# Two transformer blocks on one core: three weight strips interleaved behind four of the norms instead of two, and the fourth strip split earlier

## Chip, cores and metric

The kernel runs on one NeuronCore of a Trainium2 chip. The metric is device time in microseconds (us) for one launch. The engines are named as in the profile: PE (TensorE), DVE (VectorE), ACT (ScalarE), POOL (GpSimd) and SP, whose queue issues the weight transfers.

## The reference

One launch computes two blocks in float32 on 512 tokens of width 1024. What matters here is that four large products each follow a root-mean-square norm directly:

```python
# first block
x = x + merged @ w_mix_out
u = rmsnorm(x, norm_ffn_w)                       # norm "ffn0"
up, gate = split(u @ w_ffn_up)
x = x + (silu(causal_dwconv(up)) * gate) @ w_ffn_down
# second block, x = rmsnorm(x, norm_final_w)
h = modulate(rms_norm(x, g_ffn1), sh1, sc1)      # norm "ffn1"
x = x + 0.5 * (1 + ga1) * swiglu(h, w1_gate, w1_up, w1_down)
h = modulate(rms_norm(x, g_mix), sh2, sc2)       # norm "mix2"
x = x + (1 + ga2) * hybrid_mixer(h, w_in, b_f, g_q, g_k, w_o)
h = modulate(rms_norm(x, g_ffn2), sh3, sc3)      # norm "ffn2"
x = x + 0.5 * (1 + ga3) * swiglu(h, w2_gate, w2_up, w2_down)
```

## The kernel before

Activations are kept transposed: 8 chunks of 128 features by 512 tokens. Every weight matrix is cut into strips of 128 output columns. One strip is one *unit* `u`, and the units of the whole program are numbered in one list, `UNITS`; `U[...]` gives the first unit of a stage. A float32 product is made from three matmuls in fp32r: weights and activations are each split into a high and a low part, and `three` issues high times high, high times low and low times high. A unit with 8 chunks is therefore 24 matmuls of 128x512 into one bank of PSUM.

Each unit passes through a ring of four slots (`SLOTS`): SP loads it into `w_raw` once the unit four earlier has ended (`unit_done`), ACT rounds it into `w_hi` (`cut_hi`), DVE subtracts to get `w_lo` (`cut_lo`, which counts `lo_cut` up), and PE waits on `lo_cut`. ACT and DVE run their instructions in the written order, so a `cut_hi` or `cut_lo` stands between other work of theirs.

The result of unit `u` goes to bank `u % 2` (`ubank`). Before it starts in that bank, PE waits on `bank_read[u % 2]` until the unit two earlier has been read out. Who reads depends on the stage. Behind ffn0, ACT copies the first strip of a pair to `t_a`, DVE runs a causal convolution of three instructions on it (`conv`), ACT applies SiLU, and then DVE multiplies with the second strip (`t_b<-t_b,ps`), which frees the second strip's bank. Behind ffn1 and ffn2, ACT applies SiLU to the first strip and DVE multiplies with the second. Behind mix2 the strips are `gate_f`, then the first query strip `p0`, then the first key strip `p0+1`, the value strip `p0+2`. ACT copies `gate_f` to `t_b`, loads another function table, and casts the two halves of `p0` to `q_hi`; DVE then makes `q_lo` in two instructions and frees the bank of `p0`. PE turns the copy of `gate_f` with four transposes between `p0+1` and `p0+2`.

A norm goes over the 8 chunks: DVE makes `t_b`, ACT makes `u_hi`, DVE makes `u_lo`. Behind the four norms above, PE does not wait for all chunks: `unit_pair` takes the first two strips side by side, so each chunk that arrives feeds 6 matmuls. The third and fourth strip follow one after the other as ordinary units. Small filler matmuls (`keep_busy`) run while PE waits for the norm. Bank 7 (`AUX`) holds the sum of squares that the norm's root is made from (`rstd_set` tells that it was read). In the ffn0 stage DVE also takes chunks of the modulation weights (`mod_chunk`, `mod_acc<-mod_raw`), whose transfers SP issues between the strips (`MOD_AT`).

Of one norm, the strips are called u0, u0+1, u0+2 and u0+3 below.

Of the kernel before, what the change touches and what calls it, by code (L numbers as in the profile page):

```python
# [18 lines left out]
KC = D_MODEL // P  # L19
# [41 lines left out]
AUX = 7  # L61
# [29 lines left out]
U = {}  # L91
# [41 lines left out]
FILL = {"mix": 0, "ffn0": 1, "ffn1": 2, "mix2": 3, "heads": 4, "ffn2": 5}  # L133
SQ = {"ffn0": 0, "ffn1": 1, "mix2": 2, "ffn2": 3}
# [43 lines left out]
def two_blocks(nc, d, out):  # L178
    ctx = ExitStack()
    with ctx:  # L180
# [3 lines left out]
        def sem(name):  # L184
            return ctx.enter_context(nc.semaphore(name))


        w_hi = [sb(f"w_hi{n}", [P, KC, P], F32R) for n in range(SLOTS)]
        with ExitStack() as r0:
            w_raw = [sb(f"w_raw{n}", [P, KC, P], F32, r0) for n in range(SLOTS)]  # L190
        with ExitStack() as r0:
            w_lo = [sb(f"w_lo{n}", [P, KC, P], F32R, r0) for n in range(SLOTS)]
# [26 lines left out]
        u_hi = sb("u_hi", [P, KC, SEQ], F32R)  # L219
        u_lo = sb("u_lo", [P, KC, SEQ], F32R)  # L220
# [45 lines left out]
        ps = ctx.enter_context(nc.psum_tensor("ps", [P, 8, SEQ], F32))  # L266
# [19 lines left out]
        squared, summed, total_done, rstd_set = (sem(n) for n in ("squared", "summed", "total_done", "rstd_set"))  # L286
        normed, u_hi_set, u_lo_set = (sem(n) for n in ("normed", "u_hi_set", "u_lo_set"))
# [30 lines left out]
        def bank(b):  # L318
            return ps[:, b, :]

        def ubank(u):

            return ps[:, {U["w_o"] + 2: 3, U["w_o"] + 3: LATE_BANK}.get(u, u % 2), :]

# [80 lines left out]
        def scalar(e):  # L405
# [25 lines left out]
            def norm(which, first_unit, groups=0):  # L431
                cut_hi(first_unit + 2)
                root(which)
                if groups:
                    e.wait_ge(mod_set, groups)
                if first_unit:
                    e.wait_ge(unit_done, first_unit)
                f = FILL[which]
                n0 = [FILL[n] for n in ("ffn0", "ffn1", "mix2", "ffn2")].index(f) * KC
                for c in range(KC):  # L440
                    e.wait_ge(normed, n0 + c + 1)
                    e.activation(u_hi[:, c, :], t_b[c % 2][:, :], ACT.Identity,  # L442
                                 bias=SHIFT[which](c) if SHIFT[which] else 0.0).then_inc(u_hi_set, 1)

            def residual(u0, which=None):
                for c in range(KC):
# [42 lines left out]
            for n, c in enumerate(QKV):  # L489
                u = U["qkv"] + n  # L490
# [53 lines left out]
            for r in range(4):  # L544
                for j in range(2):
                    t = 2 * r + j
                    for s, sec in enumerate(("cc", "cx", "cb", "gc")):
                        step = 4 * j + s
                        u = U["conv"] + 4 * t + s
# [37 lines left out]
            for t in range(KC):  # L587
                u = U["merge"] + 2 * t
# [48 lines left out]
            p0 = U["proj"]  # L637
# [92 lines left out]
            u = U["gate_f"]  # L730
# [22 lines left out]
            for i in range(N_SB):  # L753
                u = p0 + 3 * (i + 1)
# [28 lines left out]
            for i in range(N_SB, N_STEPS):  # L783
                u = p0 + 3 * (i + 1)
                t = i + 1 - N_SB
# [39 lines left out]
            u0 = U[2, "down", 2]  # L825
# [8 lines left out]
        def vector(e):  # L834
# [38 lines left out]
            def norm(which, first_unit):  # L873
                f = FILL[which]
                order = [FILL[n] for n in ("ffn0", "ffn1", "mix2", "ffn2")].index(f)
                n0 = order * KC

                def low(c):
                    e.wait_ge(u_hi_set, f * KC + c + 1)
                    if SHIFT[which] is None:  # L880
                        e.tensor_tensor(u_lo[:, c, :], t_b[c % 2][:, :], f32(u_hi[:, c, :]), ALU.subtract).then_inc(u_lo_set, 1)
                    else:
                        e.scalar_tensor_tensor(out=u_lo[:, c, :], in0=t_b[c % 2][:, :], scalar=SHIFT[which](c), in1=f32(u_hi[:, c, :]),  # L883
                                               op0=ALU.add, op1=ALU.subtract).then_inc(u_lo_set, 1)

                cut_lo(first_unit + 2)
                e.wait_ge(rstd_set, SQ[which] + 1)
                e.wait_ge(summed, SQ[which] * KC + KC)
                for c in range(KC):
                    if c >= 2:  # L890
                        low(c - 2)
                        e.wait_ge(u_lo_set, f * KC + c - 1)
                    e.scalar_tensor_tensor(out=t_b[c % 2][:, :], in0=x[:, c, :], scalar=GAIN[which](c), in1=rstd[:, :],  # L893
                                           op0=ALU.mult, op1=ALU.mult).then_inc(normed, 1)
                low(KC - 2)
                low(KC - 1)

            def residual(u0, gain=None, which=None):
                for c in range(KC):
# [84 lines left out]
            for at in (0, P):  # L984

                ins = e.tensor_copy(mask_win[:, at:at + P], ones[:, :])
# [114 lines left out]
            for r in range(4):  # L1101
                for j in range(2):
                    t = 2 * r + j
                    for s, sec in enumerate(("cc", "cx", "cb", "gc")):
                        step = 4 * j + s
                        u = U["conv"] + 4 * t + s
# [30 lines left out]
            for c in range(KC):  # L1137
                u = U["conv_out"] + c
# [4 lines left out]
            for t in range(KC):  # L1143
                j = t % 2
                u = U["merge"] + 2 * t
# [66 lines left out]
            p0 = U["proj"]  # L1212
# [114 lines left out]
            for i in range(N_SB):  # L1327
                u = p0 + 3 * (i + 1)
# [21 lines left out]
            for i in range(N_SB, N_STEPS):  # L1350
                u = p0 + 3 * (i + 1)
                t = i + 1 - N_SB
# [86 lines left out]
        def tensor(e):  # L1439
# [6 lines left out]
            def three(out_, left, right, start, stop, skip=False):  # L1446
                mm(out_, left[0], right[0], start, skip, skip=skip and not start)
                mm(out_, left[0], right[1], False, skip, skip=skip)
                return mm(out_, left[1], right[0], False, stop or skip, skip=skip)

            def unit(u, acts, ready=None):
                n_k = UNITS[u][3]
                c = u % SLOTS
                e.wait_ge(lo_cut, u + 1)
                if u == U["w_o"] + OPEN_STRIPS:

                    e.wait_ge(p_cut, cuts_before(N_STEPS - 1) + 3)
                elif u >= 2:
                    e.wait_ge(bank_read[u % 2], u // 2)
                for k in range(n_k):  # L1460
                    if ready:
                        e.wait_ge(ready[0], ready[1] + k + 1)
                    ins = three(ubank(u), (w_hi[c][:, k, :], w_lo[c][:, k, :]), (acts[0][:, k, :], acts[1][:, k, :]), k == 0, k == n_k - 1)
                ins.then_inc(unit_done, 1)
# [3 lines left out]
                for _ in range(n):  # L1468
                    mm(ps[:, b, 0:2 * P], ones_r[:, :], mask_win[:, :], True, True)

            def unit_pair(u, acts, ready):

                for v in (u, u + 1):
                    e.wait_ge(lo_cut, v + 1)
                    if v >= 2:
                        e.wait_ge(bank_read[v % 2], v // 2)
                for k in range(KC):
                    e.wait_ge(ready[0], ready[1] + k + 1)
                    for v in (u, u + 1):
                        c = v % SLOTS  # L1480
                        ins = three(ubank(v), (w_hi[c][:, k, :], w_lo[c][:, k, :]), (acts[0][:, k, :], acts[1][:, k, :]), k == 0, k == KC - 1)
                        if k == KC - 1:
                            ins.then_inc(unit_done, 1)

            u_act, y_act, o_act = (u_hi, u_lo), (y_hi, y_lo), (o_hi, o_lo)
# [84 lines left out]
            u = U["qkv"] + 1  # L1570
            e.wait_ge(bank_read[u % 2], u // 2 + 1)
            for tb in range(TB):
                ins = turn(ps[:, 6, tb * P:(tb + 1) * P], v_t[:, tb * P:(tb + 1) * P])
# [76 lines left out]
            def ffn(f):  # L1650
                for part, tiles in enumerate(FF_PARTS):
                    if part == 0:
                        unit_pair(U[f, "up", 0], u_act, (u_lo_set, FILL[f"ffn{f}"] * KC))
                    for t in range(2 if part == 0 else 0, 2 * tiles):
                        unit(U[f, "up", part] + t, u_act)
                    if f == 2 and part == 2:
                        break
                    if f == 1 and part == 0:
                        mod_turn(2)
                    for c in range(KC):  # L1660
                        if f == 0 and part == 2 and c == 4:
                            mod_turn(0)
                        unit(U[f, "down", part] + c, y_act, (y_lo_set, Y_FILL[f, part]) if c == 0 else None)
                    if f == 1 and part == 0:
                        mod_turn(3)
# [30 lines left out]
            p0 = U["proj"]  # L1696
            u = U["gate_f"]
# [73 lines left out]
                k, w = HEAD_ORDER[pos], u % SLOTS  # L1771
                return three(ubank(u), (w_hi[w][:, k, :], w_lo[w][:, k, :]), (u_hi[:, k, :], u_lo[:, k, :]), pos == 0, pos == KC - 1)

            unit_pair(u, u_act, (u_lo_set, FILL["mix2"] * KC))
            unit(p0 + 1, u_act)
            e.wait_ge(bank_read[u % 2], u // 2 + 1)
            for tb in range(TB):
                ins = turn(ps[:, 6, tb * P:(tb + 1) * P], t_b[0][:, tb * P:(tb + 1) * P])
# [3 lines left out]
            for tb in range(TB):  # L1782
                dst = ps[:, 6, tb * N_FOX:(tb + 1) * N_FOX]
                for t in range(tb + 1):
                    ins = mm(dst, consts[:, C_TRIU:C_TRIU + P] if t == tb else ones[:, :], fl[:, t * N_FOX:(t + 1) * N_FOX], t == 0, t == tb)
# [3 lines left out]
            for tb in range(TB):  # L1789
                ins = turn(ps[:, 5, tb * P:(tb + 1) * P], f_wide[:, tb, :])  # L1790
            ins.then_inc(fc_turned, 1)

            for i in range(N_STEPS):
                u = p0 + 3 * (i + 1)
# [51 lines left out]
            u0 = U[2, "down", 2]  # L1846
            for c in range(KC + 1):
                if c < KC:
                    unit(u0 + c, y_act, (y_lo_set, Y_FILL[2, 2]) if c == 0 else None)
                if c:  # L1850
                    u = u0 + c - 1
# [3 lines left out]
                    for tb in range(TB):  # L1855
                        ins = turn(ps[:, 2 + (c - 1) % 4, tb * P:(tb + 1) * P], x[:, c - 1, tb * P:(tb + 1) * P])
# [27 lines left out]
```

## Time and profile before

| what | value |
|---|---|
| median of 3 runs | 1847.07 us |
| lowest, highest | 1846.68, 1847.16 us |
| the profiled execution's own time | 1847.39 us |
| its span, first to last instruction | 1845.6 us |
| PE busy | 1830.2 us (99%) |
| DVE busy | 990.5 us (54%) |
| ACT busy | 672.4 us (36%) |

Spans and starts are in microseconds from the first instruction of the profiled execution. A timeline row has the start, the duration, the engine, the line of the kernel, the operation, output and inputs, shapes, the count, and in brackets for how long the engine stood idle before it and what it then waited for. Matmuls overlap: one of 128x512 lasts 0.39 us in such a row, while the next starts earlier.

### The profile page before, as it was taken

The numbers are of one execution on the slowest core, as the hardware profiler recorded it, in microseconds if no ns is written. First come the engines' busy times: TensorE is split into PE (matmuls) and PEld (weight loads), VectorE is DVE, ScalarE is ACT, GpSimd is POOL, SyncE is SP. The second block draws the span as 40 slices with busy tenths as digits, with TensorE's granted clock in tenths as the row PEclk, the third lists the DMA queues.
The fourth block names the chain that finished last, engine by engine and source line by source line (L and its number), as shares of the span: only waits on it lengthen the run. The fifth ranks groups of instructions, "written<-read, shape, count | busy, mean of one in ns | idle before, by whom it ended". The sixth has DMA issues, their size and how long they took to land.

```text
span 1845.6 us, 20904 instructions
## 1 busy us (share of the span) xinstructions
PE 1830.2 (99%) x8645; PEld 1526.5 (83%) x8645; DVE 990.5 (54%) x1355; ACT 672.4 (36%) x1020; POOL 38.4 (2%) x73
## 2 busy tenths in 40 slices
PE   9999999999999999999999999999999999999998
PEld 8888888887888888878888888788888888888887
DVE  5655453457787756673433334666767543333333
ACT  5534441334323323252223222464666432222222
POOL 0000000000000000000000000010200000000001
PEclk9999999999999999999999999999999999999999
DMA  5222223354586555233333332312121323333323
GB/s 150 72 87 80 80 82 91 91 189 155 192 260 218 193 194 193 81 86 97 91 92 103 91 103 81 91 49 55 47 58 35 92 82 101 92 102 93 102 86 97
DMA packets 321860, 200.03 MB, mean 108 GB/s; under 512 B 6712, under 2 KB 311270, under 8 KB 321766
## 3 DMA queue, kind: packets, MB, share of 16 engines
q1 hardware_dynamic: 320882, 196.30, 35.5%
q0 software_dynamic: 640, 2.10, 0.4%
q8 instruction: 69, 1.13, 0.3%
q10 hardware_dynamic: 244, 0.30, 0.1%
q14 instruction: 25, 0.20, 0.0%
HBM read 196.57 MB, written 2.10 MB: 108 GB/s over the span
## 4 chain that ended last, share of the span: by engine, by line
PE 95%; DVE 2%; ACT 2%; DMA 1%; issue 0%; SPq 0%; POOL 0%; ACTq 0%; DVEq 0%
PE ps L1441 93%; PE ps L1444 2%; DMA w_raw<-in_w_in 0%; DVE t_b L893 0%; ACT w_hi L423 0%; DVE u_lo L883 0%; DMA w_raw<-in_w_o 0%; ACT L426 0%; DVE w_lo L851 0%; DVE u_lo L1308 0%; ACT u_hi L442 0%; DVE x L908 0%; ACT rstd L428 0%; DVE k_lo L1233 0%; DVE q_lo L1221 0%
## 5 line engine op out<-in xcount | busy, mean ns | idle before, releaser
L1441 PE MATMUL ps<-u_hi,w_hi 128*128 128x512 f32 (+1 forms) x1704 | 667.4, 392 | 4.7 <-DVE u_lo L883 1.8
L1441 PE MATMUL ps<-u_hi,w_lo 128*128 128x512 f32 (+1 forms) x1704 | 660.1, 387 | 0.0
L1441 PE MATMUL ps<-u_lo,w_hi 128*128 128x512 f32 (+1 forms) x1704 | 659.9, 387 | 0.0
L851 DVE TENSOR_TENSOR w_lo<-w_raw,w_hi 128x1024 fp32r<-128x1024 f32 (+2 forms) x307 | 364.6, 1188 | 272.8 <-ACT w_hi L423 271.9
L423 ACT ACTIVATE w_hi<-w_raw 128x1024 fp32r<-128x1024 f32 (+2 forms) x307 | 314.3, 1024 | 234.5 <-DMA w_raw<-in_w_down 79.5
L1441 PEld LDWEIGHTS ps<-u_hi,w_hi 128*128 128x128 f32 x1704 | 320.0, 188 | 76.8 <-issue 7.2
L1441 PEld LDWEIGHTS ps<-u_hi,w_lo 128*128 128x128 f32 x1704 | 319.9, 188 | 66.1
L1441 PEld LDWEIGHTS ps<-u_lo,w_hi 128*128 128x128 f32 x1704 | 320.2, 188 | 63.5 <-issue 1.2
L1441 PE MATMUL ps<-y_hi,w_hi 128*128 128x512 f32 x656 | 256.0, 390 | 0.0
L1441 PE MATMUL ps<-y_hi,w_lo 128*128 128x512 f32 x656 | 255.3, 389 | 0.0
L1441 PE MATMUL ps<-y_lo,w_hi 128*128 128x512 f32 x656 | 255.2, 389 | 0.0
L1441 PEld LDWEIGHTS ps<-y_hi,w_lo 128*128 128x128 f32 x656 | 123.1, 188 | 25.8
L1441 PEld LDWEIGHTS ps<-y_hi,w_hi 128*128 128x128 f32 x656 | 123.1, 188 | 25.3
L1441 PEld LDWEIGHTS ps<-y_lo,w_hi 128*128 128x128 f32 x656 | 123.2, 188 | 25.3
L621 ACT ACTIVATE y_hi<-t_b 128x512 fp32r<-128x512 f32 x66 | 41.7, 632 | 239.9 <-DVE t_b L1179 239.9
L908 DVE SCALAR_TENSOR_TENSOR x<-ps,gains,x 128x512 f32<-128x512 f32 x56 | 42.0, 750 | 140.2 <-PE ps L1441 140.2
L1179 DVE TENSOR_TENSOR t_b<-t_b,ps 128x512 f32<-128x512 f32 x66 | 45.2, 685 | 111.9 <-PE ps L1441 111.9
L971 DVE SCALAR_TENSOR_TENSOR mod_acc<-mod_raw,c_act,mod_acc 128x1024 f32<-128x1024 f32 x63 | 80.7, 1281 | 3.0
L618 ACT ACTIVATE t_b<-ps 128x512 f32<-128x512 f32 x44 | 26.4, 600 | 142.1 <-PE ps L1441 142.1
L1181 DVE TENSOR_TENSOR y_lo<-t_b,y_hi 128x512 fp32r<-128x512 f32 x66 | 45.7, 693 | 46.1 <-ACT y_hi L621 46.1
L453 ACT ACTIVATE t_b<-x 128x512 f32<-128x512 f32 x32 | 20.2, 632 | 98.7 <-DVE x L906 53.5
L906 DVE TENSOR_TENSOR x<-x,ps 128x512 f32<-128x512 f32 x32 | 22.0, 686 | 34.0 <-PE ps L1441 34.0
(275 smaller groups left out, 1416.0 us busy)
## 6 DMA issues: line engine op xcount, KB each, us to landing
mod_raw<-in_w_mod SPq DMA_DIRECT2D x72, 512.0 KB, 4.8
w_raw<-in_w_in SPq DMA_DIRECT2D x71, 512.0 KB, 3.8
w_raw<-in_w_ffn_up SPq DMA_DIRECT2D x44, 512.0 KB, 4.0
w_raw<-in_w_gate SPq DMA_DIRECT2D x44, 512.0 KB, 3.8
w_raw<-in_w_up SPq DMA_DIRECT2D x44, 512.0 KB, 3.8
w_raw<-in_w_down SPq DMA_DIRECT2D x32, 512.0 KB, 3.8
w_raw<-in_w_ffn_down SPq DMA_DIRECT2D x16, 512.0 KB, 4.2
w_raw<-in_w_down SPq DMA_DIRECT2D x16, 384.0 KB, 3.4
```

The source lines that it names most:

```text
L423: e.activation(w_hi[u % SLOTS][:, 0:n_k, :], w_raw[u % SLOTS][:, 0:n_k, :], ACT.Copy).then_inc(hi_cut, 1)
L453: e.activation(t_b[c % 2][:, :], x[:, c, :], ACT.Square).then_inc(squared, 1)
L618: e.activation(t_b[j][:, :], ubank(u), ACT.Silu).then_inc(bank_read[u % 2], 1)
L621: e.activation(y_hi[:, t, :], t_b[j][:, :], ACT.Copy).then_inc(y_hi_set, 1)
L851: e.tensor_tensor(w_lo[u % SLOTS][:, 0:n_k, :], w_raw[u % SLOTS][:, 0:n_k, :], f32(w_hi[u % SLOTS][:, 0:n_k, :]), ALU.subtract).then_inc(l ...
L906: ins = e.tensor_tensor(x[:, c, :], x[:, c, :], ubank(u), ALU.add)
L908: ins = e.scalar_tensor_tensor(out=x[:, c, :], in0=ubank(u), scalar=gain(c), in1=x[:, c, :], op0=ALU.mult, op1=ALU.add)
L971: e.scalar_tensor_tensor(out=acc, in0=r, scalar=c_act[:, k:k + 1], in1=acc, op0=ALU.mult, op1=ALU.add).then_inc(mod_taken, 1)
L1179: e.tensor_tensor(t_b[j][:, :], t_b[j][:, :], ubank(u + 1), ALU.mult).then_inc(bank_read[(u + 1) % 2], 1)
L1181: e.tensor_tensor(y_lo[:, t, :], t_b[j][:, :], f32(y_hi[:, t, :]), ALU.subtract).then_inc(y_lo_set, 1)
L1441: return e.matmul(out_, lhsT, rhs, start=start, stop=stop, skip_group_check=skip)
L1444: return e.transpose(out_, in_, consts[0:n, C_IDENT:C_IDENT + n])
```

## The change

`unit_pair` becomes `unit_three`: for each chunk of the activations it runs three matmuls for each of u0, u0+1 and u0+2. All 72 matmuls are the same ones as before, in another order. Since u0 and u0+2 would share a bank, the third strip (`THIRD`) now goes to bank 7, after the root has been read from it. Its count in `bank_read` is kept. At the end of `norm`, both ACT and DVE now split strip u0+3 at once; the calls that stood later in the stage find it done. Behind mix2, the split of `p0+2` already stood right behind the norm. Nothing else is altered, and the first norm of the program is left as it was.

```diff
--- before.py
+++ after.py
@@ -318,7 +318,12 @@
         def bank(b):
             return ps[:, b, :]

+
+        THIRD = {U[f, "up", 0] + 2: f"ffn{f}" for f in range(3)} | {U["gate_f"] + 2: "mix2"}
+
         def ubank(u):
+            if u in THIRD:
+                return ps[:, AUX, :]

             return ps[:, {U["w_o"] + 2: 3, U["w_o"] + 3: LATE_BANK}.get(u, u % 2), :]

@@ -441,6 +446,7 @@
                     e.wait_ge(normed, n0 + c + 1)
                     e.activation(u_hi[:, c, :], t_b[c % 2][:, :], ACT.Identity,
                                  bias=SHIFT[which](c) if SHIFT[which] else 0.0).then_inc(u_hi_set, 1)
+                cut_hi(first_unit + 3)

             def residual(u0, which=None):
                 for c in range(KC):
@@ -894,6 +900,7 @@
                                            op0=ALU.mult, op1=ALU.mult).then_inc(normed, 1)
                 low(KC - 2)
                 low(KC - 1)
+                cut_lo(first_unit + 3)

             def residual(u0, gain=None, which=None):
                 for c in range(KC):
@@ -1468,17 +1475,19 @@
                 for _ in range(n):
                     mm(ps[:, b, 0:2 * P], ones_r[:, :], mask_win[:, :], True, True)

-            def unit_pair(u, acts, ready):
-
-                for v in (u, u + 1):
+            def unit_three(u0, ready):
+
+                for v in range(u0, u0 + 3):
                     e.wait_ge(lo_cut, v + 1)
-                    if v >= 2:
+                    if v in THIRD:
+                        e.wait_ge(rstd_set, SQ[THIRD[v]] + 1)
+                    elif v >= 2:
                         e.wait_ge(bank_read[v % 2], v // 2)
                 for k in range(KC):
                     e.wait_ge(ready[0], ready[1] + k + 1)
-                    for v in (u, u + 1):
+                    for v in range(u0, u0 + 3):
                         c = v % SLOTS
-                        ins = three(ubank(v), (w_hi[c][:, k, :], w_lo[c][:, k, :]), (acts[0][:, k, :], acts[1][:, k, :]), k == 0, k == KC - 1)
+                        ins = three(ubank(v), (w_hi[c][:, k, :], w_lo[c][:, k, :]), (u_hi[:, k, :], u_lo[:, k, :]), k == 0, k == KC - 1)
                         if k == KC - 1:
                             ins.then_inc(unit_done, 1)

@@ -1650,8 +1659,8 @@
             def ffn(f):
                 for part, tiles in enumerate(FF_PARTS):
                     if part == 0:
-                        unit_pair(U[f, "up", 0], u_act, (u_lo_set, FILL[f"ffn{f}"] * KC))
-                    for t in range(2 if part == 0 else 0, 2 * tiles):
+                        unit_three(U[f, "up", 0], (u_lo_set, FILL[f"ffn{f}"] * KC))
+                    for t in range(3 if part == 0 else 0, 2 * tiles):
                         unit(U[f, "up", part] + t, u_act)
                     if f == 2 and part == 2:
                         break
@@ -1771,8 +1780,7 @@
                 k, w = HEAD_ORDER[pos], u % SLOTS
                 return three(ubank(u), (w_hi[w][:, k, :], w_lo[w][:, k, :]), (u_hi[:, k, :], u_lo[:, k, :]), pos == 0, pos == KC - 1)

-            unit_pair(u, u_act, (u_lo_set, FILL["mix2"] * KC))
-            unit(p0 + 1, u_act)
+            unit_three(u, (u_lo_set, FILL["mix2"] * KC))
             e.wait_ge(bank_read[u % 2], u // 2 + 1)
             for tb in range(TB):
                 ins = turn(ps[:, 6, tb * P:(tb + 1) * P], t_b[0][:, tb * P:(tb + 1) * P])
```

The first place is PE's queue behind the norm ffn0, where `w_hi2` and `w_hi3` are the slots of u0 and u0+1 and `w_hi0` is that of u0+2. Before:

```order
L1441 MATMUL ps<-u_hi,w_hi2 128x512 [waits bank_read1,lo_cut,u_lo_set,bank_read0]
L1441 MATMUL ps<-u_lo,w_hi2 128x512
L1441 MATMUL ps<-u_hi,w_lo2 128x512
L1441 MATMUL ps<-u_hi,w_hi3 128x512
L1441 MATMUL ps<-u_lo,w_hi3 128x512
L1441 MATMUL ps<-u_hi,w_lo3 128x512
L1441 MATMUL ps<-u_hi,w_hi2 128x512 [waits u_lo_set]
```

Now:

```order
L1448 MATMUL ps<-u_hi,w_hi2 128x512 [waits lo_cut,bank_read1,rstd_set,u_lo_set,bank_read0]
L1448 MATMUL ps<-u_lo,w_hi2 128x512
L1448 MATMUL ps<-u_hi,w_lo2 128x512
L1448 MATMUL ps<-u_hi,w_hi3 128x512
L1448 MATMUL ps<-u_lo,w_hi3 128x512
L1448 MATMUL ps<-u_hi,w_lo3 128x512
L1448 MATMUL ps<-u_hi,w_hi0 128x512
L1448 MATMUL ps<-u_lo,w_hi0 128x512
L1448 MATMUL ps<-u_hi,w_lo0 128x512
L1448 MATMUL ps<-u_hi,w_hi2 128x512 [waits u_lo_set]
```

Nine matmuls, not six, stand between one wait for `u_lo_set` and the next. Strip u0+3 still comes behind the same 72 matmuls and still waits on `lo_cut` and `bank_read1`.

The second place is DVE's queue behind the same norm, from its last `u_lo` to the product of the first pair of strips. Before:

```order
L881 TENSOR_TENSOR u_lo<-t_b1,u_hi 128x512 [waits u_hi_set]
L1200 TENSOR_TENSOR w2e<-vec 128x8
L1201 TENSOR_SCALAR w2e<-w2e 128x8 [waits dve_own]
L977 TENSOR_SCALAR t_b0<-t_a0,vec 128x512 [waits bank_read0,dve_own]
L978 SCALAR_TENSOR_TENSOR t_b0<-t_a0,vec,t_b0 128x512 [waits dve_own]
L979 SCALAR_TENSOR_TENSOR t_b0<-t_a0,vec,t_b0 128x512 [waits dve_own]
L851 TENSOR_TENSOR w_lo1<-w_raw1,w_hi1 128x1024 [waits hi_cut]
L1179 TENSOR_TENSOR t_b0<-t_b0,ps 128x512 [waits hidden_act,unit_done]
L1181 TENSOR_TENSOR y_lo<-t_b0,y_hi 128x512 [waits y_hi_set]
```

Now:

```order
L887 TENSOR_TENSOR u_lo<-t_b1,u_hi 128x512 [waits u_hi_set]
L857 TENSOR_TENSOR w_lo1<-w_raw1,w_hi1 128x1024 [waits hi_cut]
L1207 TENSOR_TENSOR w2e<-vec 128x8
L1208 TENSOR_SCALAR w2e<-w2e 128x8 [waits dve_own]
L984 TENSOR_SCALAR t_b0<-t_a0,vec 128x512 [waits bank_read0,dve_own]
L985 SCALAR_TENSOR_TENSOR t_b0<-t_a0,vec,t_b0 128x512 [waits dve_own]
L986 SCALAR_TENSOR_TENSOR t_b0<-t_a0,vec,t_b0 128x512 [waits dve_own]
L1186 TENSOR_TENSOR t_b0<-t_b0,ps 128x512 [waits hidden_act,unit_done]
L1188 TENSOR_TENSOR y_lo<-t_b0,y_hi 128x512 [waits y_hi_set]
```

The split of u0+3 (slot 1) stood between the convolution and the product and now stands ahead of the convolution. ACT's queue changes alike: `w_hi1` moves from behind the SiLU to right behind the last `u_hi`.

## Rows read from the trace of the kernel before

**Rows 1.** Page, busy time by engine, and clock granted in 40 slices
```profile
PE 1830.2 (99%) x8645; PEld 1526.5 (83%) x8645; DVE 990.5 (54%) x1355; ACT 672.4 (36%) x1020; POOL 38.4 (2%) x73
...
PEclk9999999999999999999999999999999999999999
```

**Rows 2.** Chain that ended last: start us, us, what
```profile
429.66 11.31 PE ps L1441 x48
441.08 5.68 PE ps L1441 x24
446.77 326.69 PE ps L1441 x1440
```

**Rows 3.** Timeline, PE: first pair matmul, fourth strip's first (three norms)
```profile
799.72 0.47 PE L1441 MATMUL ps<-u_hi,w_hi 128*128 128x512 f32 x1
...
817.21 0.39 PE L1441 MATMUL ps<-u_hi,w_hi 128*128 128x512 f32 x1
...
1171.70 0.47 PE L1441 MATMUL ps<-u_hi,w_hi 128*128 128x512 f32 x1 [0.92 <-DVE u_lo L883]
...
1189.32 0.47 PE L1441 MATMUL ps<-u_hi,w_hi 128*128 128x512 f32 x1
...
1476.26 0.47 PE L1441 MATMUL ps<-u_hi,w_hi 128*128 128x512 f32 x1 [0.92 <-DVE u_lo L883]
...
1493.52 0.39 PE L1441 MATMUL ps<-u_hi,w_hi 128*128 128x512 f32 x1
```

**Rows 4.** Timeline behind ffn0's norm: PE, then ACT, then DVE
```profile
439.90 0.39 PE L1441 MATMUL ps<-u_hi,w_lo 128*128 128x512 f32 x1
...
440.33 0.60 ACT L612 ACTIVATE t_a<-ps 128x512 f32<-128x512 f32 x1 [2.42 <-PE ps L1441]
...
443.19 0.63 ACT L614 ACTIVATE t_b<-t_b 128x512 f32<-128x512 f32 x1 [0.96 <-DVE t_b L979]
...
442.40 0.75 DVE L979 SCALAR_TENSOR_TENSOR t_b<-t_a,vec,t_b 128x512 f32<-128x512 f32 x1
...
445.94 0.68 DVE L1179 TENSOR_TENSOR t_b<-t_b,ps 128x512 f32<-128x512 f32 x1
```

**Rows 5.** Timeline behind mix2's norm: ACT, then DVE
```profile
1182.68 0.60 ACT L734 ACTIVATE t_b<-ps 128x512 f32<-128x512 f32 x1 [1.38 <-PE ps L1441]
...
1185.83 1.39 DVE L1221 SCALAR_TENSOR_TENSOR q_lo<-ps,q_hi 64x512 fp32r<-64x512 f32 x2 [3.27 <-ACT q_hi L644]
```

**Rows 6.** Timeline behind ffn2's norm: ACT, then DVE
```profile
1487.23 0.60 ACT L618 ACTIVATE t_b<-ps 128x512 f32<-128x512 f32 x1 [0.15 <-PE ps L1441]
...
1489.95 0.68 DVE L1179 TENSOR_TENSOR t_b<-t_b,ps 128x512 f32<-128x512 f32 x1
```

**Rows 7.** Timeline, DVE: two norm products of ffn1, one chunk apart
```profile
801.06 0.75 DVE L893 SCALAR_TENSOR_TENSOR t_b<-x,gains,rstd 128x512 f32<-128x512 f32 x1
...
802.51 0.75 DVE L893 SCALAR_TENSOR_TENSOR t_b<-x,gains,rstd 128x512 f32<-128x512 f32 x1
```

**Rows 8.** DMA issues at 440.33, 441.36, 810.73 and 1182.67: us to landing
```profile
w_raw<-in_w_ffn_up SPq DMA_DIRECT2D x1, 512.0 KB, 4.1
...
w_raw<-in_w_ffn_up SPq DMA_DIRECT2D x1, 512.0 KB, 6.5
...
w_raw<-in_w_gate SPq DMA_DIRECT2D x1, 512.0 KB, 3.9
...
w_raw<-in_w_in SPq DMA_DIRECT2D x1, 512.0 KB, 4.7
```

**Rows 9.** Timeline behind ffn1's norm: ACT, then DVE
```profile
817.90 1.05 ACT L423 ACTIVATE w_hi<-w_raw 128x1024 fp32r<-128x1024 f32 x1
...
818.99 1.23 DVE L851 TENSOR_TENSOR w_lo<-w_raw,w_hi 128x1024 fp32r<-128x1024 f32 x1 [1.41 <-ACT w_hi L423]
```

**Rows 10.** Timeline, PE: filler matmuls at the start and in ffn0's norm
```profile
3.23 6.23 PE L1441 MATMUL ps<-mask_win,ones_r 128*128 128x256 f32 x30 [3.23 <-DVE mask_win L986]
...
425.01 3.91 PE L1441 MATMUL ps<-mask_win,ones_r 128*128 128x256 f32 x28
```

## The prediction

> **What bounds the kernel now.** I read the page first. PE is busy 1830.2 of 1845.6 us and its granted clock is full in every slice [rows 1]. So nearly every delay of PE is a delay of the end, and there are only 15 us without PE work in the whole program to gain from. The chain that ended last shows the same at ffn0: 48 matmuls of the pair, 24 of the third strip, then 1440 without a break [rows 2]. Off the norms a matmul takes 326.69 / 1440 = 0.2269 us. The total work does not change, so only four places matter, one behind each norm. For each I compare two times: from the first matmul of the pair (call it t0) to the first matmul of strip u0+3. The reader should see in the rows that this is 446.77 - 429.66 = 17.11 us for ffn0 [rows 2], and 17.49, 17.62 and 17.26 us for ffn1, mix2 and ffn2 [rows 3].
>
> **What the change can gain.** DVE delivers a chunk every 1.45 us behind ffn1 (802.51 - 801.06) [rows 7], and a pair uses it in 6 x 0.2269 = 1.36 us, so PE waits a little for each. Three strips need 2.04 us for a chunk and never wait. The third strip also no longer waits for bank `u0 % 2` to be read. The triple's own length: the pair's 48 matmuls last 11.31 us to the end of the last one [rows 2]; less 0.39 us for that last matmul's own length [rows 4], 47 intervals took 10.92 us. That was in the norm's time with DVE and ACT at work, so I keep it, and take 0.2269 us for the rest. The matmul after the triple could then start at t0 + 10.92 + 25 x 0.2269 = t0 + 16.59. Alone, this would gain 0.52 us at ffn0, 0.90 at ffn1, 0.67 at ffn2 and at most 17.62 - 16.59 = 1.03 at mix2, where four transposes still stand in between.
>
> **What the change moves closer.** Strip u0+3 uses the bank of u0+1 and waits until that was read. Before, PE had the whole of u0+2 (5.68 us [rows 2]) to cover the reading. Now u0, u0+1 and u0+2 end within 6 matmuls of each other, 1.36 us. Call the end of u0's last matmul E. It is the 66th of the triple: E = t0 + 10.92 + 18 x 0.2269 + 0.39 = t0 + 15.39. The reading starts at E, so its length now stands open, from what PE can cover (t0 + 16.59, that is E + 1.20) on.
>
> *ffn0.* Before, u0 ended at 439.90 + 0.39 = 440.29. ACT copied at 440.33, the convolution ended at 442.40 + 0.75 = 443.15, SiLU ran from 443.19 to 443.82 [rows 4]. The split of u0+3 stood next, and the product came at 445.94 and took 0.68. With the split gone to an earlier, empty place, the product starts one hop of 0.04 us after SiLU, 443.86, and ends at 444.54. PE started 446.77 - 446.62 = 0.15 us after the product's end before [rows 2, 4], so 444.69: E + 4.40. Strip u0+3 starts at t0 + 19.79, against 17.11: **+2.68 us**. The split moved early was worth doing, since without it this would be about 2.1 us longer, but it doesn't undo the wait.
>
> *mix2.* `gate_f` is u0 and `p0` is u0+1. Before, `gate_f` ended 0.04 us before ACT's copy at 1182.68, at 1182.64; behind it come a table load, two casts, and the two `q_lo`, which end at 1185.83 + 1.39 = 1187.22 [rows 5]. That is 4.58 us, and with the hop of 0.15 to PE 4.73. Nothing of it was moved. `p0+2` starts at t0 + 15.39 + 4.73 = 20.12, against 17.62: **+2.50 us**. The transposes lie inside the wait.
>
> *ffn1 and ffn2.* The chain is short. SiLU takes 0.60 us; the product can't start before u0+1 ends, 0.68 us after E, and a hop; it takes 0.68 [rows 6]. So the bank is free at E + 1.40 and PE goes on at E + 1.55 = t0 + 16.94. Against 17.49 and 17.26: **-0.55** and **-0.32 us**. I take rows of ffn2 for both; ffn1 has more reductions on DVE, but they follow the norm directly and have the whole triple to run beside, so I give them nothing.
>
> **The fifth strip.** u0+4 takes the slot of u0, so its load starts at E and was covered by 11 us of PE; now 7.1 us are left (E + 1.55 + 24 x 0.2269 + 0.1). The load lands 3.9 us after issue at ffn1 [rows 8], `w_hi` and `w_lo` take 818.99 + 1.23 - 817.90 = 2.32 us [rows 9], and hops 0.2: E + 6.4. It fits with 0.7 us to spare, at cost nothing. If it didn't, the cover is u0+3 and every tenth more is paid in full. At ffn0 and mix2 the stall above gives more room (loads of 4.1 and 4.7 us against 9.9 us). At ffn0 the load had three more behind it in the queue and still took 4.1, while that of u0+5 took 6.5 [rows 8]; so later transfers hardly delay the first. The Trainium skill (DMA: Bandwidth & Descriptors, Queues, rings and completion order) says that descriptors of one ring are consumed in ring order; the trace agrees, and by it u0+4 stays the first served, though now three loads start within 1.4 us. Other moved work costs nothing: the early split of u0+3, one ACT and one DVE instruction, runs while PE has the last chunk and more of the triple still to do. PE's three waits at its start, among them that for bank 7, are all over before the first `u_lo`.
>
> **Sum.** 2.68 + 2.50 - 0.55 - 0.32 = +4.31 us. Behind each place PE is the limit again and no idle time is left to absorb it. On the profiled execution that is 1847.39 + 4.3 = 1851.7. Its own time is 0.3 above the median of the runs, so the median becomes 1847.07 + 4.3 = **1851.4 us**. The likeliest case's own range, from 0.2 us of error in each of eight starts and the fillers' and restarts' small change, is 1850.3 to 1853.0.
>
> **The rivals.**
> - *Part of the loss comes back.* A wait later in the program that another engine sets would not move with PE. For it: behind ffn0 DVE's chain of splits, convolutions and chunks is nearly as long as PE's, and behind mix2 much waits on engines other than PE. Against it: all these chains start from PE's ends. If 0.7 to 1.8 us came back, the sum is +2.5 to +3.6, 1849.6 to 1850.7. Chance 0.17.
> - *The fifth strip is late.* If its load lands as late as the second in a burst did, 6.5 us [rows 8], the split ends 2.6 - 0.7 = 1.9 us too late at ffn1 and ffn2 each: +3.8, 1855.2. Decides from a landing above 4.6 us. Chance 0.07.
> - *The clock falls.* PE would stand idle for 4.40 - 1.36 = 3.0 us at ffn0 and some 2.8 us at mix2. PE's idle times behind the norms are now 0.92 us at most in my rows [rows 3]. At the start, after 3.23 us of idling, 30 fillers took 6.23 us, 0.208 each, while 28 of the same shape took 3.91 us in the norm, 0.140 each [rows 10], though the granted clock is shown as full there too. If each wait threw PE to 1.2 GHz for the same 6.2 us, 3.1 us of work would be lost at each: +6.2, 1857.6. The Trainium skill (TensorE: Matmul & The Clock Gate, Part 1) says "the default state is throttled, and activity releases the throttle"; no row here shows it inside the program. Chance 0.06.
> - *The wait does not bind, and it gets faster.* If u0+1's bank were free within E + 1.2 everywhere, the gains of the second paragraph stand alone: 0.52 + 0.90 + 1.03 + 0.67 = 3.1 at most, 1844.0. It decides where the reading takes under 1.2 us; the rows show 4.40 and 4.73. Chance 0.04.
>
> **How the numbers follow.** My forecast has 0.66. A measurement of this kernel can tell about 0.2%, 3.7 us. The forecast, the late strip and the clock are above it (0.79), the partly returned loss within (0.17), the rival without the wait below (0.04). The range reaches from the second case to the late strip, 1849.5 to 1855.3, and leaves the clock and the gain out.
>
> **What the profile after would show.** PE idle some 3 us before strip u0+3 of ffn0, released by DVE's product (`t_b<-t_b,ps`), and before `p0+2` of mix2, released by `q_lo`; about 0.35 us at ffn1 and ffn2; no waits for `u_lo` between chunks; the start of u0+3 at t0 + 19.8, 16.9, 20.1 and 16.9. I am wrong if either long wait is missing, if PE waits for `w_lo` at u0+4, or if matmuls behind a wait take longer than 0.2269 us.

## The result and the profile after

The changed kernel takes 1854.48 us in the median of 6 runs (1852.99 to 1856.62), the kernel before 1847.07 (1846.68 to 1848.46). The ratio is 1.0040, with a 95% interval of 1.0027 to 1.0053. It is slower by 7.4 us, where 4.3 was forecast. The profiled execution took 1854.44 us, its span is 1852.7, 7.1 longer than before.

The page's busy times:

```profile
PE 1831.4 (99%) x8645; PEld 1530.9 (83%) x8645; DVE 990.9 (53%) x1355; ACT 672.6 (36%) x1020; POOL 38.3 (2%) x73
```

The waits of PE (us in total, times, longest):

```profile
PE ps L1448 <- DVE t_b L1186: 3.6, 3, 3.1
...
PE ps L1448 <- DVE q_lo L1228: 2.9, 1, 2.9
```

The page row answers to that of [rows 1]: busy time grew by 1.2 us and the span by 7.1. The waits for `t_b` (the product of the first pair of strips, with 3.1 of the 3.6 us at ffn0) and for `q_lo` are new.

Next is the chain that ended last (start us, us, what), at ffn0 and then at mix2:

```profile
429.51 15.26 PE ps L1448 x66
444.79 0.61 ACT t_a L618
...
447.65 0.64 ACT t_b L620
448.38 0.70 DVE t_b L1186
449.21 328.18 PE ps L1448 x1440
...
1175.14 15.23 PE ps L1448 x66
...
1193.54 0.68 DVE q_lo L1228
1194.23 0.70 DVE q_lo L1228
1195.07 9.47 PE ps L1448 x44
```

Read it as a relay. The triple's 66 matmuls up to u0's end are on the chain. Then the chain leaves PE for ACT and DVE, which it never did here before [rows 2]: copy, convolution, SiLU, product. PE comes back at 449.21. At mix2 it leaves for the casts and `q_lo`. The next rows are PE's timeline at the starts of u0+3, and the start of the triple of ffn1 (803.66):

```profile
803.66 0.47 PE L1448 MATMUL ps<-u_hi,w_hi 128*128 128x512 f32 x1
...
820.52 0.47 PE L1448 MATMUL ps<-u_hi,w_hi 128*128 128x512 f32 x1 [0.25 <-DVE t_b L1186]
...
1195.07 0.47 PE L1448 MATMUL ps<-u_hi,w_hi 128*128 128x512 f32 x1 [2.92 <-DVE q_lo L1228]
...
1500.42 0.47 PE L1448 MATMUL ps<-u_hi,w_hi 128*128 128x512 f32 x1 [0.21 <-DVE t_b L1186]
```

The triples of mix2 and ffn2 begin at 1175.14 and, in the same chain, at 1483.61:

```profile
1483.61 15.94 PE ps L1448 x69
```

| from t0 to the start of u0+3, us | before | forecast | after |
|---|---|---|---|
| ffn0 | 17.11 | 19.79 | 19.70 |
| ffn1 | 17.49 | 16.94 | 16.86 |
| mix2 | 17.62 | 20.12 | 19.93 |
| ffn2 | 17.26 | 16.94 | 16.81 |

These add up to +3.82 us, not to 7.1. Most of the rest shows between one norm and the next. From t0 of ffn0 to t0 of ffn1 it was 370.06 us and is 374.15, 4.09 more, of which the wait explains 2.59. From mix2 to ffn2 it was 304.56 and is 308.47, 3.91 more, of which the wait explains 2.31. So 1.50 and 1.60 us are lost right behind the waits; the last 0.2 us are small differences elsewhere. What the 1.50 and 1.60 are, the table of stretches shows (us, PE busy and count, granted clock, DMA share, GB/s), first behind ffn0, then behind mix2:

```profile
448.00:449.00 1.00, 0.00 (x0) 1.00 1.04 416
449.00:450.00 1.00, 0.79 (x2) 0.51 1.05 340
...
451.00:452.00 1.00, 1.00 (x4) 0.50 1.01 377
...
453.00:454.00 1.00, 1.00 (x6) 1.00 1.22 308
...
1193.00:1194.00 1.00, 0.00 (x0) 1.00 1.15 341
...
1195.00:1196.00 1.00, 0.93 (x4) 1.00 1.19 287
...
1197.00:1198.00 1.00, 1.00 (x4) 0.50 0.18 43
1198.00:1199.00 1.00, 1.00 (x4) 0.50 0.00 0
...
1200.00:1201.00 1.00, 1.00 (x6) 1.00 0.00 0
```

About when PE begins again, or a little after, the granted clock falls from 1.00 to 0.50, from 2.4 to 1.2 GHz, for about 3 us, and is full again after that. Matmul by matmul:

```profile
449.21 0.76 PE L1448 MATMUL ps<-u_hi,w_hi 128*128 128x512 f32 x1 [3.10 <-DVE t_b L1186]
...
450.20 0.63 PE L1448 MATMUL ps<-u_hi,w_lo 128*128 128x512 f32 x1
450.63 0.63 PE L1448 MATMUL ps<-u_hi,w_hi 128*128 128x512 f32 x1
...
454.91 0.39 PE L1448 MATMUL ps<-u_hi,w_hi 128*128 128x512 f32 x1
455.14 0.39 PE L1448 MATMUL ps<-u_lo,w_hi 128*128 128x512 f32 x1
```

At half clock one starts every 0.43 us (450.20, 450.63), at full clock every 0.23 (454.91, 455.14).

### The profile page after: what moved, and what is told of

Read it like the earlier page. It is cut to its first block, busy times and chain, and to the rows that moved or that the text cites. A ratio compares the mean times of both kernels' runs of the same rounds, so it can differ in the third digit from the quotient of the medians.

```text
span 1852.7 us, 20903 instructions
## 1 busy us (share of the span) xinstructions
PE 1831.4 (99%) x8645; PEld 1530.9 (83%) x8645; DVE 990.9 (53%) x1355; ACT 672.6 (36%) x1020; POOL 38.3 (2%) x73
## 4 chain that ended last, share of the span: by engine, by line
PE 96%; DVE 2%; ACT 2%; issue 0%; DMA 0%; POOL 0%; ACTq 0%; DVEq 0%; POOLq 0%
PE ps L1448 94%; PE ps L1451 2%; ACT w_hi L428 0%; DVE q_lo L1228 0%; DMA w_raw<-in_w_o 0%; ACT L431 0%; DVE u_lo L1315 0%; ACT q_hi L650 0%; DVE x L915 0%; DVE k_lo L1240 0%; DVE w_lo L857 0%; DVE t_b L899 0%; ACT att_a L694 0%; ACT u_hi L447 0%; DVE t_b L1186 0%
```

## The experiments

The first four ran together on one chip, the last four together on another, each four with the kernel before beside them; times are medians of 7 to 11 runs. The kernel before took 1847.19 us beside the first four (27 runs) and 1847.03 beside the last four (31 runs). "t0" is again the first matmul behind a norm.

### Fillers over the two waits (e1_fill)

```diff
 unit_three(U[f, "up", 0], (u_lo_set, FILL[f"ffn{f}"] * KC))
+if f == 0:
+    keep_busy(20)
...
 ins.then_inc(f_turned, 1)
+keep_busy(18)
 unit(p0 + 2, u_act)
```

> The changed kernel with 20 small filler matmuls on PE between the triple and strip u0+3 of ffn0, and 18 between the four transposes and p0+2 of mix2; nothing else. My theory: the loss has two parts, the waits for the bank of u0+1 to be read (2.59 and 2.31 us in the changed kernel's trace) and a stretch at half clock behind each of them (1.5 and 1.6 us). The fillers don't shorten the waits but keep PE at work, so the half-clock part goes and the waits stay: 1854.5 - 3.1 = about 1851.3 us, granted clock full behind both places, strip u0+3 still at t0 + 19.7 and p0+2 at t0 + 19.9. Rival: the clock falls for another reason than PE's idle time (the burst of loads that runs at the same moment): then the half-clock rows stay and the time is 1854.5.

Measured: 1851.19 us, ratio 1.0022 (1.0013 to 1.0031), +4.0. PE's timeline at ffn0, from t0 on:

```profile
429.62 0.47 PE L1448 MATMUL ps<-u_hi,w_hi 128*128 128x512 f32 x1 [0.74 <-DVE u_lo L887]
...
446.02 2.55 PE L1448 MATMUL ps<-mask_win,ones_r 128*128 128x256 f32 x20
449.30 0.47 PE L1448 MATMUL ps<-u_hi,w_hi 128*128 128x512 f32 x1 [0.72 <-DVE t_b L1186]
```

And the granted clock in the same stretch (the value behind the counts):

```profile
440.00:480.00 40.00, 39.28 (x184) 1.00 0.62 198
```

Strip u0+3 starts 449.30 - 429.62 = 19.68 us after t0, so the wait is as long as it was; 20 fillers fill it up to 0.72 us. The same holds at mix2, where 18 fillers leave 0.79 us of idling and p0+2 starts at t0 + 19.94. The clock stays full at both places, and 3.3 of the 7.4 us are gone, although the loads burst as before. What is left, 4.0, is about what the four starts give, 3.82. So PE's idle time takes the clock down here, and the rival is out.

### Only the short reading chains (e2_only_f12), only ffn0 (e3_only_f0), only mix2 (e4_only_mix)

```diff
-THIRD = {U[f, "up", 0] + 2: f"ffn{f}" for f in range(3)} | {U["gate_f"] + 2: "mix2"}
+THIRD = {U[f, "up", 0] + 2: f"ffn{f}" for f in (1, 2)}        # e3: (0,);  e4: mix2 alone
...
-    if part == 0:
+    three_up = part == 0 and f in (1, 2)                      # e3: (0,);  e4: ()
+    if three_up:
         unit_three(U[f, "up", 0], (u_lo_set, FILL[f"ffn{f}"] * KC))
+    elif part == 0:
+        unit_pair(U[f, "up", 0], u_act, (u_lo_set, FILL[f"ffn{f}"] * KC))
...
-unit_three(u, (u_lo_set, FILL["mix2"] * KC))                  # e2 and e3, at mix2; e4 keeps it
+unit_pair(u, u_act, (u_lo_set, FILL["mix2"] * KC))
+unit(p0 + 1, u_act)
```

> Three strips side by side behind ffn1 and ffn2 only; behind ffn0 and mix2 the pair, as in the kernel before; the early split of the fourth strip stays everywhere. My theory: only the short reading chains are here, so the change gains 0.63 and 0.45 us at the two starts of u0+3, some 0.1 of it lost at each restart, and at ffn0 the early split takes away the 0.17 us wait of u0+3: 1847.07 - 0.9 = 1846.2 us. Rival: the early split or the fifth strip costs something at ffn1 and ffn2, and the time is 1847 or more.

> Three strips side by side behind ffn0 only, pairs elsewhere. My theory: one long wait (2.6 us) and one stretch at half clock (1.5 us): 1847.07 + 4.1 = 1851.2 us. Rival without a clock part: 1849.7. Rival with the clock falling for longer in some runs: 1852 and more, with more spread than the kernel before.

> Three strips side by side behind mix2 only, pairs elsewhere. My theory: one long wait (2.3 us) and one stretch at half clock (1.6 us), less the 0.17 us that the early split saves at ffn0: 1847.07 + 3.7 = 1850.8 us. If the four places are independent, the differences of this run, the ffn0 one and the ffn1 and ffn2 one add up to the change's own +7.1 to +7.4. Rival: something outside the four places costs time only when all are changed, and the three add up to less than 6.

| three strips at | expected us | measured us | ratio (95%) |
|---|---|---|---|
| ffn1, ffn2 | 1846.2 | 1845.81 | 0.9994 (0.9985 to 1.0003) |
| ffn0 | 1851.2 | 1852.47 | 1.0026 (1.0015 to 1.0037) |
| mix2 | 1850.8 | 1852.80 | 1.0026 (1.0016 to 1.0036) |

The last two are slower, as expected, but 1.3 and 2.0 us above what I wrote. The first has the sign that I expected, but its interval includes no change; its starts of u0+3 show the gain better: 16.83 us after t0 at ffn1 and 16.78 at ffn2, before 17.49 and 17.26. One microsecond of each is in the waits of PE, in a place that I had not looked at. In e3_only_f0 the pair is back at ffn1, and PE waits there for ACT (its waits):

```profile
PE ps L1448 <- ACT t_b L624: 1.3, 1, 1.3
```

ACT's timeline has the table load and the SiLU that PE waits for:

```profile
814.62 1.28 ACT L624 ACT_TABLE_LOAD   x1
815.92 0.60 ACT L624 ACTIVATE t_b<-ps 128x512 f32<-128x512 f32 x1
```

At ffn1, ACT has to make the root of the plain sum and load a table before the SiLU of u0, on which the pair's third strip waits. The early split of u0+3 now stands ahead of all that; u0+3 starts 18.45 us after t0, before 17.49. Under the triple the same delay is hidden, since u0 ends later: in the changed kernel's trace ACT waits 3.15 us for PE before this SiLU. The second part is the clock: in e4_only_mix the stretch from mix2 to ffn2 took 309.81 us, 1.3 more than with the change, with an equally long wait. The granted clock around mix2:

```profile
1160.00:1200.00 40.00, 35.83 (x165) 0.91 0.26 66
```

Read microsecond by microsecond, the clock fell at 1191.4, in the wait, and was full again only at 1198.2: some 7 us at half clock, where the change had about 3. The fall cost 309.81 - 304.56 - 2.33 = 2.92 us here. How much a fall costs differs from one execution to another.

The three differences, -1.4, +5.3 and +5.6, add up to 9.5; without the 1 us that two of them owe to the pair at ffn1 it is 7.6, against 7.4 for the change. Each of the three is known to about 2 us only, so the sum agrees with four independent places but doesn't prove them. The traces say it more sharply: with three strips at one place alone u0+3 starts at t0 + 19.67 (ffn0) and t0 + 19.95 (mix2), as in the changed kernel.

### u0+1 in a bank of its own (e5_fresh)

```diff
+FRESH = (U[0, "up", 0] + 1, U["gate_f"] + 1)
 def ubank(u):
+    if u in FRESH:
+        return ps[:, 2, :]
...
-    e.wait_ge(bank_read[u % 2], u // 2)
+    e.wait_ge(bank_read[u % 2], u // 2 - (u - 2 in FRESH))
```

> The changed kernel, with strip u0+1 of ffn0 and of mix2 in a bank of its own (bank 2), so that u0+3 no longer waits for u0+1 to be read. My theory of the two long waits: they are the reading of that bank and nothing else, so u0+3 of ffn0 starts at t0 + 16.6 and p0+2 at t0 + 16.9. But what lay behind them comes next: at ffn0 the low part of strip u0+4 stands on DVE behind two chunks of the modulation (it ended 24.7 us after t0 in the changed kernel), so PE waits 2.6 us there; at mix2 the logarithm chain of the gate ends at about t0 + 23.7, 1.3 us after PE needs it. Net against the kernel before: +2.2 at ffn0, +0.6 at mix2, -1.1 at ffn1 and ffn2: +1.7, 1848.9 us, and up to 1.5 more if 2.6 us of waiting also halves the clock. Rival: the bank is not what holds PE, and the long waits stay where they are: 1854.5.

Measured: 1852.16 us (1849.34 to 1854.27), ratio 1.0025 (1.0016 to 1.0035). In the profiled execution u0+3 starts at t0 + 16.42 and p0+2 at t0 + 16.79, without a wait. PE's waits are now these (3.7 us are 2.7 here and 1.0 at the program's start, as before):

```profile
PE ps L1452 <- DVE w_lo L861: 3.7, 2, 2.7
...
PE ps L1452 <- DVE gate L1330: 1.4, 1, 1.4
```

The first in PE's timeline:

```profile
454.17 0.80 PE L1452 MATMUL ps<-u_hi,w_hi 128*128 128x512 f32 x1 [2.69 <-DVE w_lo L861]
```

The stretches around both, with the granted clock:

```profile
452.00:453.00 1.00, 0.00 (x0) 1.00 1.05 323
...
455.00:456.00 1.00, 1.00 (x3) 0.50 1.05 337
...
1197.00:1198.00 1.00, 0.01 (x1) 1.00 0.01 2
...
1202.00:1203.00 1.00, 1.00 (x5) 0.50 0.00 0
```

So the bank was all that held PE at these two places, and the next link was as late as computed: 2.69 us for the low part of u0+4 (expected 2.6), 1.42 us for the gate's logarithm (expected 1.3). The fastest run, with a mean clock of 1.000, took 1849.34, close to the 1848.9 without a clock part. I had allowed one fall, up to 1850.4; the profiled execution has two, and the median lies 1.8 us above that bound. Taking away this one wait does not make the triple pay at these places: PE finds the next link late, and the clock falls again.

### No fillers in the norms of the kernel before (e6_no_fill)

```diff
-keep_busy(16)
 total("ffn0")
-keep_busy(28)
...
-keep_busy(16)
 total("mix2")
-keep_busy(28)
```

> The kernel before (pairs), without the filler matmuls in the norms ffn0 and mix2 (16 and 28 at each). No wait is made longer, since PE waits for the norm there anyway; PE only stands idle in it, for some 4.6 us behind the total and 2 us ahead of it. If idle time alone halves the clock, as the runs with and without fillers over the waits of the changed kernel say, the first matmuls of each pair run at half clock, and 1.5 to 3 us are lost at each of the two norms: 1850 to 1853 us. Part of it may be hidden, as the pair waits for DVE's chunks at full clock. Rival: the clock falls only together with the burst of loads behind a triple, and the time stays at 1847.1.

Measured: 1852.18 us, ratio 1.0026 (1.0016 to 1.0035), +5.2. PE behind ffn0's norm:

```profile
429.63 0.77 PE L1441 MATMUL ps<-u_hi,w_hi 128*128 128x512 f32 x1 [4.08 <-DVE u_lo L881]
...
431.05 0.63 PE L1441 MATMUL ps<-u_hi,w_hi 128*128 128x512 f32 x1
431.47 0.63 PE L1441 MATMUL ps<-u_lo,w_hi 128*128 128x512 f32 x1
```

PE starts at the same moment as with fillers [rows 2], but at half clock, 0.42 us a matmul. The granted clock around ffn0's norm, then around mix2's, then further behind mix2:

```profile
424.00:432.00 8.00, 3.50 (x8) 0.62 0.35 120
...
1172.00:1176.00 4.00, 3.06 (x7) 0.50 0.02 4
...
1198.00:1204.00 6.00, 6.00 (x37) 0.72 0.33 90
```

No bank, no strip and no load is different here, so idle time brings the clock down without a triple and without its burst of loads. At each of the two norms the clock was at half for some 7 us, part of it while PE stood idle anyway: u0+3 starts 18.37 us after t0 at ffn0 (before 17.11) and 18.96 at mix2 (before 17.62), 1.26 and 1.34 us lost. The third row is a fall that I had not expected. It lasts about 3 us and costs the other 1.6 of the 4.2 us by which this profiled execution is longer, and PE was busy all the time ahead of it, for 2.1 us with matmuls only 8 columns wide. The kernel before runs the same matmuls there at full clock. Why the clock fell in one and not in the other, no run here shows.

### The early split alone (e7_early)

```diff
 # kernel before, at the end of norm, on ACT and on DVE
+cut_hi(first_unit + 3)
...
+cut_lo(first_unit + 3)
```

> The kernel before (pairs) with the early split of the fourth strip alone. Behind ffn1 the split stands in ACT's queue ahead of the root of the plain sum, the table load and the SiLU of u0, on which the pair's next strip waits; in the runs with a pair at ffn1 that wait grew from 0.28 to 1.3 us and u0+3 started at t0 + 18.45, not 17.49. So +0.96 at ffn1, -0.17 at ffn0, nothing at mix2 and ffn2: 1847.07 + 0.8 = 1847.9 us. Rival: those two runs owed the 1 us to something else, and this one gives 1846.9.

Measured: 1848.12 us, ratio 1.0005 (0.9996 to 1.0014). In its trace u0+3 of ffn1 starts 18.42 us after t0, where it was 17.49, and u0+3 of ffn0 16.94, where it was 17.11. The median moved by 1.1, the trace says 0.8; the change of the median is not clear of the noise, but both starts moved as expected. So the early split costs a pair at ffn1 0.9 us.

### Where it is free, and only there (e8_best)

```diff
 # e2_only_f12 with THIRD for all four places, and in unit:
+elif u in THIRD:
+    e.wait_ge(rstd_set, SQ[THIRD[u]] + 1)
 elif u >= 2:
     e.wait_ge(bank_read[u % 2], u // 2)
```

> Three strips side by side at ffn1 and ffn2 only, pairs at ffn0 and mix2; there the third strip goes to bank 7 too and doesn't wait for u0 to be read. The run with three at ffn1 and ffn2 only gave 1845.8, 1.4 below the kernel before. The third strip's wait of 0.26 us at ffn0 and 0.26 us at mix2 goes as well: 1845.3 us. Rival: the wait only moves on to u0+3, whose bank is read no sooner, and the time stays at 1845.8.

Measured: 1845.21 us, ratio 0.9988 (0.9979 to 0.9997), 1.8 us below the kernel before and as expected. The interval is just clear of no change; the 0.6 us against e2_only_f12 is not clear of the noise by the medians, and rests on the starts in the traces. In its trace u0+3 starts at t0 + 16.61, 16.83, 17.26 and 16.81: shorter than before at all four, and at ffn0 and mix2 shorter than the 16.91 and 17.62 of e2_only_f12. This is the fastest version found.

## Why the prediction was right, and where it was not

- *What bounds it, and what a triple gains.* Right. The starts of u0+3 at ffn1 and ffn2 are within 0.13 us of the forecast, there are no waits between chunks, and e2_only_f12, expected to gain 0.9 us, gained 1.4 by its median, though its interval includes no change.
- *The reading of u0+1's bank.* Right, in place and length: 19.70 and 19.93 us against 19.79 and 20.12. The bank as the cause is shown by e5_fresh.
- *The fifth strip.* Right. No wait for `w_lo` at u0+4. The load of u0+4 at ffn0 landed after 3.9 us, before 4.1 [rows 8], with three behind it:

```profile
w_raw<-in_w_ffn_up SPq DMA_DIRECT2D x1, 512.0 KB, 3.9
```

- *The step that failed* is the term that the sum left out: the rival "the clock falls", which I gave 0.06, because no row showed it inside the program. The clock falls at both long waits, and my own sign of being wrong, matmuls behind a wait that take longer than 0.2269 us, came true: 0.43 us. I took 6.2 us of half clock and 3.1 us of loss for each place; in the profiled execution it was about 3 us and a loss of 1.50 and 1.60, in e4_only_mix some 7 us and 2.92. The evidence I had was [rows 10], the slow fillers behind 3.23 us of idling, and the forecast waits were nearly as long as that. e1_fill and e6_no_fill show the fall from both sides. The Trainium skill (TensorE: Matmul & The Clock Gate, Part 1) says that the default state is throttled and that activity releases the throttle. These two runs agree with the second half, full clock with fillers and 0.50 without; on the default state they show nothing.
- *Luck.* Forecast plus the clock, 4.3 + 3.1 = 7.4, is what the medians give, but not so exactly: in the profiled execution the starts give 3.82, not 4.31. And the measured 1854.48 lies inside the range of 1849.5 to 1855.3 only because its upper end was set by the late fifth strip, which didn't happen. The likeliest case's own range ended at 1853.0, and the clock's case, 1857.6, was left out.
- *"Behind each place PE is the limit again."* Right. Nothing came back: with the clock held up by fillers (e1_fill) the loss is 4.0 us, and the starts give 3.82. The rival of a partly returned loss is out.
- *"Other moved work costs nothing."* True under the triple, but not by itself: at ffn1 the early split costs a pair 0.9 us (e7_early), since ACT's queue there has the root and a table load to do first.

## What to carry to other kernels

When units are interleaved, their results all come due at once. Work out from the end of the first one how long its readers take, and compare that with what the tensor engine still has in hand; a bank more for the third unit doesn't help if the fourth needs the second's. Then price any wait of some microseconds on a busy tensor engine twice, as the wait and as the half-clock stretch that can come with it (1.5 to 2.9 us for waits of about 3 us here), and where the wait can't be removed, put fillers over it.

## What the runs showed of the hardware that I had not expected

- The clock fell in or behind waits of 3.10, 2.92 and 2.69 us. In e5_fresh it fell too after 1.42 us of idling followed by matmuls only 8 columns wide, and only almost 3 us after PE had begun again; in e6_no_fill it fell behind the same narrow matmuls with no idling just ahead of them. With 20 fillers and 0.72 us of idling left it did not fall. Nor did it in the last 4.8 us of the kernel before, in which PE stands idle and the granted clock is 1.00. So these rows make a fall likely behind a wait of about 3 us, and no rule for when it comes.
- It need not fall during the wait. At ffn0 it was down when PE began again; at mix2 PE had run for more than 1 us at full clock before; at mix2 of e4_only_mix it fell inside the wait. Nor is its length fixed: about 3 us in one, some 7 in the other. What a fall costs varies with it, and that is probably why the change's six runs lie as far apart as 1852.99 us (mean clock 0.999) and 1856.62 (0.996).
- The kernel before probably has a fall in some runs as well: beside the last four experiments five of its 31 runs stand at 1848.3 to 1848.8, all with a mean clock of 0.999, and most others near 1847.0. No profile here caught one of them, so where in the program it would be is open. A mean clock of 0.999 alone proves nothing: e8_best's profiled execution has it, and its clock falls only in the last 3 us, behind PE's last matmul.
